# The first input projection of a hybrid encoder step by seven block products, with x written out meanwhile

## What is computed

```python
mod = jax.nn.silu(c) @ ada_w[layer] + ada_b[layer]
sh_m, sc_m, g_m, sh_f, sc_f, g_f = jnp.split(mod[:, None, :], 6, axis=-1)
h = rms_norm(x, norm_mix_w[layer]) * (1.0 + sc_m) + sh_m
proj = h @ w_in_ab[j]
# columns 0:1792 go to rwkv7_mixer: p + (previous token's p - p) * mu
# then z (1024 columns), x/B/C (1536: a convolution of width 4 over tokens, SiLU), dt (16)
mix = jnp.concatenate([oa, ob], axis=-1) @ w_out_ab[j]
x = x + g_m * mix
```

## Time and profile before

| | us |
|---|---|
| median of 3 runs | 3676.99 |
| lowest, highest | 3674.79, 3683.19 |
| profiled execution | 3683.28 |
| its span, first to last instruction | 3681.5 |
| first projection, first cast to its last matmul | 35.2 to 536 |
| second projection, first cast to its last matmul | 2061.8 to 2454.5 |

### The profile page before, as it was taken

One profiled execution on the slowest core, in us unless ns is written; L12 is line 12 of the kernel. 1 busy time (PEld: TensorE's weight loads), 2 busy tenths in 40 slices (PEclk: granted clock), 3 DMA queues, 4 the chain that ended last, 5 costly groups with the idle time before them and its releaser, 6 DMA issues. The chain is left out here.

```text
span 3681.5 us, 69547 instructions
## 1 busy us (share of the span) xinstructions
PE 3492.0 (95%) x29505; PEld 3282.6 (89%) x29505; DVE 2152.3 (58%) x3107; ACT 1150.9 (31%) x1973; POOL 1583.6 (43%) x1261
## 2 busy tenths in 40 slices
PE   8999987998989899999999899989979999999998
PEld 6999976777669899999999799987769899999998
DVE  6443656764984755555544845547766755555446
ACT  3000115663640333333200444435541433332100
POOL 4222222220012377777433378840033677776331
PEclk9999998999999999999999999999989999999999
DMA  7454540103331122222322133333351122223322
GB/s 234 160 187 154 182 138 25 33 24 81 80 101 43 32 72 72 70 69 71 123 89 73 62 126 120 124 122 100 100 158 55 54 72 72 69 69 117 96 88 75
DMA packets 396908, 349.04 MB, mean 95 GB/s; under 512 B 20275, under 2 KB 363857, under 8 KB 391486
## 3 DMA queue, kind: packets, MB, share of 16 engines
q1 hardware_dynamic: 391024, 323.93, 28.3%
q10 hardware_dynamic: 5454, 20.73, 1.4%
q0 software_dynamic: 128, 0.02, 0.2%
HBM read 254.68 MB, written 89.96 MB: 94 GB/s over the span
## 5 line engine op out<-in xcount | busy, mean ns | idle before, releaser
L1513 PE MATMUL ffn_acc<-ffn_BH,ffn_WH 128*128 128x384 f32 x1232 | 418.7, 340 | 23.5 <-DVE ffn_BL L1725 12.6
L1513 PE MATMUL ffn_acc<-ffn_BL,ffn_WH 128*128 128x384 f32 x1232 | 417.1, 339 | 0.0
L1513 PE MATMUL ffn_acc<-ffn_BH,ffn_WL 128*128 128x384 f32 x1232 | 416.7, 338 | 0.0
L1448 POOL TENSOR_TENSOR ffn_WL<-raw,ffn_WH 128x512 fp32r<-128x512 f32 x176 | 282.8, 1608 | 260.9 <-ACT ffn_WH L1599 260.9
L1942 PE MATMUL ffn_acc<-ffn_BH,ffn_WH 128*128 128x384 f32 x1056 | 354.4, 336 | 5.7 <-DVE ffn_BL L2006 4.3
L1942 PE MATMUL ffn_acc<-ffn_BL,ffn_WH 128*128 128x384 f32 x1056 | 354.2, 335 | 0.0
L675 PE MATMUL in_ab_acc<-hH,in_ab_wH 128*128 128x384 f32 (+2 forms) x840 | 288.0, 345 | 3.4 <-ACT hH L518 3.4
L1448 POOL TENSOR_TENSOR ffn_WL<-ffn_S,ffn_WH 128x512 fp32r<-128x512 f32 x176 | 274.5, 1570 | 33.8 <-ACT ffn_WH L1599 33.8
L675 PE MATMUL in_ab_acc<-hL,in_ab_wH 128*128 128x384 f32 (+2 forms) x840 | 282.7, 339 | 0.0
L1513 PEld LDWEIGHTS ffn_acc<-ffn_BH,ffn_WH 128*128 128x128 f32 x1232 | 234.2, 190 | 31.1 <-POOL ffn_WL L1448 14.6
L2015 DVE SCALAR_TENSOR_TENSOR xT<-ffn_acc,mod,xT 128x768 f32<-128x768 f32 x96 | 97.6, 1016 | 255.3 <-PE ffn_acc L1942 255.3
(11 more groups left out here) (686 smaller groups left out, 8739.4 us busy)
## 6 DMA issues: line engine op xcount, KB each, us to landing
spare<-in_ada_w SPq DMA_DIRECT2D x42, 1024.0 KB, 5.1
hidden<-ffn_up SPq DMA_DIRECT2D x44, 576.0 KB, 2.8
raw<-in_w_gate SPq DMA_DIRECT2D x44, 512.0 KB, 3.8
raw<-in_w_up SPq DMA_DIRECT2D x44, 512.0 KB, 3.8
raw<-in_w_down SPq DMA_DIRECT2D x80, 256.0 KB, 2.7
pT<-in_ab_out ACTq DMA_DIRECT2D x34, 576.0 KB, 3.4
raw<-in_w_in_ab SPq DMA_DIRECT2D x34, 512.0 KB, 4.9
raw<-in_w_in_c SPq DMA_DIRECT2D x32, 512.0 KB, 4.0
```

The lines of the kernel that those rows point to most:

```text
L1448: self.nc.gpsimd.tensor_tensor(self.WL[:, slot], src, self.WH[:, slot].bitcast(F32), ALU.subtract).then_inc(lo, 1)
L1513: ins = self.nc.tensor.matmul(self.acc[:, bank, 0:n], w[:, slot, k, :], x(low, k), start=start and k == 0 and w is self.WH and low == 0, s ...
```

## The change

The first projection takes the scheme of `Mixed`, as a subclass `FirstMixed`: 17 pairs of tiles in the order RWKV (14 tiles), x/B/C (12), gates (8); then the remainder of 16 columns from the blocks at hand, 84 matmuls. The third chunk of the first pair is multiplied without its 10 shift columns, then the shift products, their turn and the 10 columns follow (`shift_part`). The blocks of x are all that is kept of it on chip: SP writes x to `hidden` during the first pair, and its room takes `cols`, `work`, the results (`projected`), `ada_rows` and the mixers' masks and small constants, which Pool now makes in pairs 3 to 8 instead of in the prologue. `mixer_out` reads x back for the first output projection as it did for the second. The modulation steps stand in three slots a pair, one step in each, behind far1, p3 and far2. Shifts are added by ScalarE (Identity with a bias) instead of VectorE. Stores are issued by SP. The first result of a gate pair is formed in `projected` itself.

```diff
-        ring = Ring(nc, g, ph, KD)
-        acc, mult, used = ring.acc, ring.mult, ring.used
-        cols, work = g.cols, g.work
-        out = ph.sb("out", [P, 2, T])
-        norm = Norm(nc, g, ph, ring, 0, 0, None, tail=False, room=out[:, 0, :])
...
-            norm.first_tiles(pe, shift_products, shift_turn, lambda: pe.wait_ge(sh_mod, 1))
-            for n in range(2, NAB + 1):
-                ring.multiply(pe, n // 2, n % 2, KD, g.hH, g.hL, rows=P if n < NAB else rest, wide=True)
-                later.multiply(pe, n)
...
-            waiting = None
-            for n in range(NAB):
-                u = n % 2
-                if n in later.ended:
-                    later.take_rows(act, later.ended[n])
-                if n in GATE:
-                    if waiting is not None:
-                        put(waiting)
-                        waiting = None
-                    act.wait_ge(norm.taken, n - JZ + 1)
-                    nc.scalar.activation(out[:, u, :], out[:, u, :], ACT.Silu).then_inc(gate_done, 1)
-                    act.wait_ge(gate_done, n - JZ + 1)
-                    store(n)
-                    continue
-                halo(n)
-                if waiting is not None:
-                    put(waiting)
-                waiting = n
...
+        self.slot_of = [first + i + i // KD for i in range(self.n)]
+        self.step_at = {slot: i for i, slot in enumerate(self.slot_of)}
...
+    def pe_first(self, pe):
+        mixed, far, nc, g = self.mixed, self.far, self.nc, self.g
+        pe.wait_ge(self.a11_lo, 1)
+        mixed(2, BX, B11, stop=False, before=lambda k: pe.wait_ge(self.b_lo, k + 1)).then_inc(self.p1_mm, 1)
+        pe.wait_ge(self.a12_lo, 1)
+        mixed(3, BY, B21, before=lambda k: pe.wait_ge(self.b_lo, HALF + k + 1)).then_inc(self.p2_mm, 1)
+        pe.wait_ge(self.ms_lo, 1)
+        self.far_tokens(pe, 2, 0, True)
+        pe.wait_ge(self.sh_zero, 1)
+        pe.wait_ge(g.shift_in, 16 * KD // 2)
+        for n in range(KD // 2):
+            products_of_halves(nc, g, self.acc[:, BSUM, :], (g.shift_w + self.rooms)[n], n).then_inc(self.sh_done, 1)
+        self.far_tokens(pe, 3, 1, False)
+        pe.wait_ge(self.sh_rows, 1)
+        for q in range(4):
+            ins = nc.tensor.transpose(self.acc[:, BSUM + 1, q * P:(q + 1) * P], self.rows[:, q * P:(q + 1) * P], g.ident[:, :])
+        ins.then_inc(self.sh_turned, 1)
+        pe.wait_ge(self.shift_lo, 1)
+        self.shift_part(2, 0, True).then_inc(self.far1a_mm, 1)
+        self.shift_part(3, 1, False).then_inc(self.far1_mm, 1)
...
+        act.wait_ge(self.sh_done, KD // 2)
+        nc.scalar.copy(self.rows, self.acc[:, BSUM, :]).then_inc(self.sh_rows, 1)
+        weigh(0, 0)
+        self.take_p1(act, 0)
+        act.wait_ge(self.sh_mod, 1)
+        for a, n in ((CH, SEQS), (CH + SEQS, SHIFTS - SEQS)):
+            ins = nc.scalar.copy(self.hH[:, :, a:a + n], self.sh[:, :, 0:n])
+        ins.then_inc(self.shift_hi, 1)
+        self.direct(B22, 1, 1)
+        self.of_difference(act, T1, 0)
...
+        dve.wait_ge(self.sh_turned, 1)
+        first, second = halves_turned(self.acc[:, BSUM + 1, :])
+        add_half(nc, g, 0, first, None).then_inc(self.sh_summed, 1)
+        dve.wait_ge(self.sh_summed, 1)
+        add_half(nc, g, 0, second, g.mod).then_inc(self.sh_mod, 1)
+        dve.wait_ge(self.shift_hi, 1)
+        for a, n in ((CH, SEQS), (CH + SEQS, SHIFTS - SEQS)):
+            ins = tt(self.hL[:, :, a:a + n], self.sh[:, :, 0:n], self.hH[:, :, a:a + n].bitcast(F32), ALU.subtract)
+        ins.then_inc(self.shift_lo, 1)
+        dve.wait_ge(self.diff_half, 1)
+        self.minus_diff(diff, 0, 1)
...
+    sequence = list(RWKV) + list(XBC_) + list(GATE)
...
+            def store(p):
+                n, u = sequence[p], p % 2
+                if n in RWKV:
+                    sp.wait_ge(mixed_, p + 1)
+                elif n in XBC_:
+                    sp.wait_ge(silu_done, p - NA + 1)
+                else:
+                    sp.wait_ge(biased, p + 1)
+                sp.dma_start(g.pT[n * P:(n + 1) * P, HALO:HALO + T], out[:, u, :]).then_inc(stored[u], 16)
...
+            m.load2(sp, 0, columns(0, 1))
+            for i, k in enumerate(range(KD // 2, KD, 2)):
+                sp.dma_start(m.rooms[i], ada[:, 0, k:k + 2, 0:D]).then_inc(g.shift_in, 16)
+            for k in range(KD):
+                sp.dma_start(g.hidden[k * P:(k + 1) * P, :], g.xT[:, k, :]).then_inc(parked, 16)
+            m.load1(sp, 1, columns(1, 0))
+            m.load2(sp, 1, columns(1, 1))
+            for j in range(1, N):
+                if j == 1:
+                    sp.wait_ge(spare_free, 1)
+                later.load(sp, ada, 3 * j - 1)
+                store(2 * j - 2)
+                later.load(sp, ada, 3 * j)
+                store(2 * j - 1)
+                if j + 1 < N:
+                    m.load1(sp, j + 1, columns(j + 1, 0))
+                else:
+                    sp.wait_ge(m.s3_set, N)
+                    sp.dma_start(g.raw[:, 0, :, 0:rest], src[:, :, NAB * P:IN_AB]).then_inc(rest_in, 16)
+                later.load(sp, ada, 3 * j + 1)
+                if j + 1 < N:
+                    m.load2(sp, j + 1, columns(j + 1, 1))
...
+            masks_of_pair = {3: set_reset, 4: set_ones64, 5: lambda: set_upto(g.before, 1), 6: lambda: set_upto(g.notafter, 0),
+                             7: set_after, 8: set_whole}
+            m.pool_first(pool)
+            for j in range(1, N):
+                m.pool_group(pool, j, masks_of_pair.get(j))
...
+                m.pe_group(pe, j, lambda n: later.multiply(pe, 3 * j + n))
...
+            of_chunk = (((block_of(B11),), (block_of(B21),)), ((block_of(B11), block_of(T1)), (block_of(B22),)), ((far,), (far,)))
...
+            def place_free(j, u):
+                if gate_pair(j):
+                    act.wait_ge(stored[u], 16 * j)
+                elif j:
+                    act.wait_ge(taken, 2 * (j - 1) + u + 1)
...
+            def add_bias_of(j, u):
+                n, p = tile_at(j, u), 2 * j + u
+                act.wait_ge((m.near1, m.near2)[u], j + 1)
+                act.wait_ge((m.far1_added, m.far2_added)[u], j + 1)
+                if n in GATE:
+                    nc.scalar.activation(out[:, u, 0:TP], out[:, u, 0:TP], ACT.Silu, bias=bias[:, u, 0:1])
+                    nc.scalar.activation(out[:, u, TP:T], out[:, u, TP:T], ACT.Silu).then_inc(biased, 1)
+                    return
+                before = seq(cols[:, u], HALO + TP)[:, :, 0:HALO]
+                if n in RWKV:
+                    copy(before[:, :, HALO - 1], g.shiftT[:, n, :]).then_inc(copied, 1)
+                else:
+                    copy(before, g.convT[:, n - JX, :].rearrange("p (s c) -> p s c", c=TAIL)).then_inc(copied, 1)
+                v = cols[:, u, HALO:HALO + TP]
+                nc.scalar.activation(v, v, ACT.Identity, bias=bias[:, u, 0:1]).then_inc(biased, 1)
+
+            def put(p):
+                if not NA <= p < first_gate:
+                    return
+                n, u = sequence[p], p % 2
+                i = n - JX
+                act.wait_ge(conv_done, i + 1)
+                act.wait_ge(stored[u], 16 * (p // 2))
+                at = ROW_B["conv_b"] + i
+                nc.scalar.activation(out[:, u, 0:TP], work[:, u, 0:TP], ACT.Silu, bias=g.colB[:, at:at + 1])
+                nc.scalar.activation(samples(out[:, u]), seq(work[:, u], HALO + TP)[:, :, 0:LS], ACT.Silu,
+                                     bias=g.colB[:, at:at + 1]).then_inc(silu_done, 1)
...
+                def after_s2():
+                    add_bias_of(j - 1, 1)
+                    put(2 * j - 2)
+                    later.take_rows(act, 3 * j - 1)
+
+                def after_s4():
+                    later.take_rows(act, 3 * j)
+
+                def at_end():
+                    put(2 * j - 1)
+                    later.take_rows(act, 3 * j + 1)
+                if j > 1:
+                    m.act_ahead(act, j)
+                    add_bias_of(j - 1, 0)
+                    take_u3(j - 1)
+                    m.act_second(act, j)
+                else:
+                    take_u3(0)
+                    m.act_second(act, 1)
+                    add_bias_of(0, 0)
+
+                def free1(act, j):
+                    sums_at(j)
+                    place_free(j, 0)
+                m.act_group(act, j, free1, after_s2, after_s4, at_end)
...
+            dve.wait_ge(parked, 16 * KD)
+            nc.vector.memset(cols, 0.0).then_inc(cleared, 1)
+            dve.wait_ge(cleared, 1)
+            place_first(0)
+            place_first(1)
+            dve.wait_ge(m.near1, 1)
+            dve.wait_ge(m.near2, 1)
+            dve.wait_ge(m.far2_added, 1)
+            dve.sem_inc(spare_free, 1)
+            finish(0)
+            for j in range(1, N):
+                finish(2 * j - 1)
+                sums_at(j)
+                later.take_mod(dve, 3 * j - 1)
+                far_of(j, 0)
```

(72 more changed lines are left out.)

770 lines of the change are left out of this document (403 added, 367 removed).

## The result

The changed kernel takes 3718.4 us (median of 4 runs, 3711.4 to 3722.6) against 3677.9 (4 runs) of the kernel before: 1.0107 times as long, 95% interval 1.0085 to 1.0129. The forecast was 3674.3, the range 3659 to 3697: the measured time lies 21 us above the range. The profiled execution took 3721.96, its span 3720.2, so 38.7 more than the profiled one of before.

A forecast was written before the change was run, and what follows sets the result against it. TensorE, busy 95% of the span, was taken to bound the kernel. -28.0 + 14.4 + 3.5 + 7.4 = -2.7 us gave 3674.3 against the median 3676.99, range 3659 to 3697.

The forecast's parts named there:

- Pairs in steady state: First projection: 16 pairs at 23.21 us plus modulation steps and the remainder, 436.4 against 464.4 before: -28.0 us.
- The remainder: Last 16 columns of the first projection: 84 matmuls at 0.1758 us, 14.8 us, where 72 took 12.6 before.
- The mix and gate pairs: First projection outside the convolutions: 26 to 27 us each, TensorE without idle time; mixes cost nothing, uncovered up to 2 us.
- First pair: Start of the first projection: 50.7 us instead of 36.37, +14.4, as ScalarE waits for the shift modulation's products.
- Second pair (pair 1): First projection: clearing columns and placing tiles delays the casts; low part ready at 12 us, wanted at 8.5; +3.5 (0 to 6).
- Convolution pairs: First projection, tiles of pairs 7 to 12: 3.0 us over five pairs, 4.4 once in pair 13; +7.4 (0 to 30).
- The wait for p1: Pairs 8 to 13: TensorE idle before T2's product until ScalarE copies p1, 0 to 1 us, 4 in the last.
- The chain: Convolution pairs, weights' landing to copy of p1: from -4.9 ends at 8.8 alone, 12.8 to 14 beside Pool; wanted at 11.8.
- B: Rival, chance 0.27: VectorE and Pool take turns, convolution pairs take some 31.5 instead of 26.9 us, six lose 30; 3697.
- "At nothing", the masks of Pool: Masks moved from the prologue into Pool's pairs 3 to 8: cost nothing; uncovered, 2 us a pair.
- a gap in a mix pair because a queue is late: Sign of being wrong, first projection: gaps in mix pairs would mean SP's or Pool's queue, costed at nothing, is late.
- Wrong if the granted clock after the start falls below 1.00: Sign of being wrong: the forecast counted matmuls at granted clock 1.00, the 2.4 GHz level, after the start.

## Why the prediction was wrong, step by step

By size, these steps failed: the effect of the shared class on other stages, which had no term (19.6); the convolution pairs, where Pool was not slowed in the sum (12.3 too little); the loads in the moved step, put at nothing (5.3); and the second pair (4.7 too little).

- **Pairs in steady state: right.** Forecast 23.21 and 1.255 a step: 26.98 with three steps; measured 26.9, without idle time (26.70 with the two columns back, so a part of this close fit is luck). The remainder: forecast 14.8, measured 14.9 (pair 16 and the remainder are 41.1, less a pair of 26.2). The mix and gate pairs other than 1, 3 and 13 cost nothing, as said.
- **First pair: right, in size and place.** Forecast 50.7, measured 50.70; ScalarE waits 9.2 for the products, 9 were forecast; VectorE starts the first difference 23.5 us in, forecast 23.6; and the run with the products moved shortens the pair.
- **Second pair (pair 1): too small.** +3.5 forecast (0 to 6), 8.2 measured. The first late low part was there (1.6 of idle time). Missing were two more stops (0.7 and 2.8) behind VectorE's mixes and Pool's low parts, which were priced at 1.3 to 1.4 each and took mostly 2.2 to 2.4, and 3.1 at the lower clock. How much each of them makes was not isolated.
- **Convolution pairs: mechanism in part, size wrong.** Forecast +7.4, measured 19.7. The wait for p1 came as forecast: 0.9 in pairs 10 to 12 (0 to 1 forecast), 4.7 in pair 13 (4.4). The chain left out T1's product, which waits for a sum that stands behind the even tile's convolution in VectorE's queue (1.2 to 1.4 in pairs 11 to 13), and Pool's low parts. The next pair's first weights were cast 2.1 to 2.6 us ahead of it, where the chain had 4.9. B said that the two engines take turns, and its sign came true (convolution operations at 2.23), but its 4.6 to 5 a pair for six pairs was too much: 0 and 0.6 in pairs 8 and 9, 3.1 to 3.5 in pairs 10 to 12. The 31.5 a pair behind it can't be worked out again from the terms that the prediction gives. In the forecast only VectorE was slowed, by the earlier trace rows; Pool stayed at 1.30 an operation. The trace of before had Pool's side too, in a group of the second projection, 2130 to 2400 us, that takes 2.03 on average (1.28 in the gate pairs after the change):

```profile
L1455 POOL TENSOR_TENSOR in_c_S<-raw 128x512 f32<-128x512 f32 x12 | 24.3, 2025 | 0.0
```

- **"At nothing", the masks of Pool: wrong.** The step of pair 3 issues four loads, and of a moved step every DMA counts; 5.3 us, not 2, and by another way than the one uncovered there. The prediction's own sign for it, a gap in a mix pair because a queue is late, came true in pair 3.
- **Not in the sum at all: the two columns in the shared class.** They stand in the diff, and the prediction has no term for them; they cost 19.6 in three other stages and some 2.3 in the clean pairs of this one (0.25 in each of nine). With them back the kernel takes 3699.0, still above the forecast by 25, and just above the range.
- **What the sum leaves out as a kind: the clock behind a stop.** "Wrong if the granted clock after the start falls below 1.00" came true: some 8 of the 33.2 us lost in the pairs are matmuls at 1.2 GHz in pairs 1, 3 and 13.
- **Right at nothing:** x is written out and read back without a stop in the first output projection (864 matmuls, 152.12 us, all of them busy).

The sum: the forecast's -2.7, 19.6 and 2.3 for the columns, 5.3 for pair 3, 4.7 for pair 1 and 12.3 for the convolutions make +41.5; the 4.5 that the mixers take less leave 37.0, against 38.7 in the profiled executions. Those 4.5 are no gain that can be counted on: from the first projection's last matmul to the first of the feed-forward stage it is 709.6 us after the change and 712.0 before, but 708.1 to 712.2 in the runs that differ from the changed kernel only ahead of it; the second mixer's products span 265.9 and 269.2, and 265.5 to 269.4 in those runs.

## What to carry to other kernels

An edit in a class that other stages share, even of unused columns, moves the buffers of all of them: list every buffer's start before and after, and cost each stage whose starts move. When a step is moved into a busy stretch, its small DMAs can cost more than its instructions; read what they took where they stood. Where two engines slow each other, cost both sides. A stop of TensorE can be paid twice, once as idle time and once at the lower clock behind it (5.1 and 3.1 us in pair 1), so a forecast of stops needs a term for that.

## What the hardware showed that I had not expected

- **The place of the weight tiles.** In the first feed-forward stage the matmuls slow down by 1.3 to 1.6% when the weight tiles begin 128 bytes further on (1156 against 1138 to 1141 matmuls in 200 us at a granted clock of 1.00; the stage 809.07 against 817.57). At 32 bytes there is no difference in the second feed-forward stage, at 64 one of 0.2% in the second projection. The Trainium skill (SBUF — State Buffer, section Who interferes with whom) gives TensorE two read ports, one for the moving operand and one for the weights, independent of each other. It says nothing of where an operand begins; these runs show that this matters, and why is not shown.
- **Small packets.** Four loads of 20 KB together took 25% of the 16 DMA engines' time over 30 us, and a weight tile was there 17.3 us after its issue; without them Pool had it after 8.8 us and did not wait.
- **The clock.** The same three stops (5.1 us in all, the longest 2.8, in pair 1) were followed by a fall of the granted clock in one execution (0.89, 32.1 us) and not in another (1.00, 29.4 us).
- **One input beside Pool.** VectorE's operation with one SBUF input took 1528 ns on average beside Pool in the convolution pairs, 832 before (the operation with two inputs 2232 and 1444). The same section of the Trainium skill exempts such operations from the contention with GpSimd only outside VectorE's two-port modes; whether this one runs in such a mode no run here shows.
